# Ten rounds of both feed-forward gate and up products as seven block products of 256 tokens in place of eight

## The chip, the cores and the metric

The kernel runs on one core of one Trainium2 chip. Its time is device microseconds; that of the kernel before is 1849.38 us, the median of three runs from 1849.03 to 1849.63 us. The engines are TensorE (PE: matmuls, weight loads), VectorE (DVE), ScalarE (ACT), GpSimd (POOL) and the DMA queues, of which SyncE (SP) issues the weight loads. Each follows its own list of instructions, and semaphores tie the lists together.

## The reference

A first block of two token mixers is followed by a second block, in which two feed-forward layers enclose a hybrid mixer and a cross attention. There are 512 tokens of width 1024, in float32. What the change touches is the first half of both feed-forward layers:

```python
def swiglu(x, w_gate, w_up, w_down):
    return (jax.nn.silu(x @ w_gate) * (x @ w_up)) @ w_down
```

The argument `x` is the residual stream normed by its root mean square and scaled by a gain per feature; `w_gate` and `w_up` are 1024 x 2816. The output has the shape of the residual stream. In each of the two layers the gate and up products are 22 column tiles of 128 each.

## The kernel before, in words

All activations lie with features on the 128 partitions and tokens along the free dimension (512). A float32 product is made of three fp32r products: a number is a high part (rounded to fp32r) and a low part (the number less its high part), and high x high, high x low and low x high are summed in PSUM.

One round of the gate and up stage computes one gate tile and one up tile of 128 features: it loads 1 MB of weights (16 tiles of 128 x 128, eight of `w_gate` and eight of `w_up`) into one of two buffers `RAW`, in four units of four tiles. For each unit `split_unit` has GpSimd write the high part (L305) and the low part (L307) into one of four slots of `weights_hi` and `weights_lo`; a slot is free again once TensorE has used its unit. `feature_tile` on TensorE takes two units for the gate bank (L411 to L413: eight k-tiles, three products each, 512 columns) and two for the up bank, so a round has 48 products; rounds alternate between two pairs of PSUM banks. The pair of the first round is computed by `tile_pair`.

Behind TensorE, `dve_ffn_up` multiplies the gate bank (L1122) and the up bank (L1124) by the rms rows `RB`, ScalarE takes the silu of the gate (L1112), VectorE multiplies both (L1127), ScalarE rounds the result to its high part `Y_H` (L1114) and VectorE subtracts for the low part `Y_L` (L1129). The banks are free after L1122 and L1124. SP loads the weights of round r+2 into a buffer once all four low parts of round r are written (`units_ready`). There are 22 such rounds in each layer: about 596 to 838 us in the first, and 1476 to 1720 us in the second, with the products with `w_down` behind them.

At the head of the first layer, `dve_between` works out the rms rows and then norms the residual stream itself (L1480, eight instructions), and ScalarE writes `RB` (L576). At the head of the second, `RB` is written at the same place, and the first silu has to load an activation table first. The order of work is that of the program text on each engine; nothing plans it at run time.

## Time and profile before

| what | value |
|---|---|
| median of three runs | 1849.38 us |
| span of the profiled execution, first to last instruction | 1847.5 us |
| TensorE busy / its weight loads | 1821.5 us (99%) / 1491.6 us |
| GpSimd busy | 1257.9 us (68%) |
| VectorE busy / ScalarE busy | 885.0 us (48%) / 510.3 us (28%) |
| mean granted clock of TensorE | 0.996 of full speed |

The profiled execution has its span as its own time; no other total is given for it, and the median of the runs is 1.9 us above that span. A matmul's duration in the profile runs from its start to its modelled end and overlaps with the next one's, so the pace of TensorE is read from the distance of two starts and not from the duration.

### The profile page before, as it was taken

The page shows a single profiled execution, that of the slowest core. Times are in us where ns is not written, and L with a number is a line of the kernel's source. Part 1 is how long each engine was busy: PE and PEld are TensorE (multiplying, and loading weights), DVE is VectorE, ACT ScalarE, POOL GpSimd, SP SyncE. Part 2 cuts the span into 40 slices and gives each one's busy share as a digit, 9 for nine tenths or more (in the row PEclk, how much of TensorE's full clock was granted, in tenths as well). Part 3 has the DMA queues.
Part 4 walks back from the last instruction along what each step waited for, and adds up shares of the span by engine and source line. Part 5 has one row for each costly group of instructions (what it writes and reads, how often), then busy time and mean ns, then how long its engine had stood idle before and what let it go on. Part 6 is the DMA issues. An engine that isn't in the chain of part 4 may idle for free.

```text
span 1847.5 us, 25864 instructions
## 1 busy us (share of the span) xinstructions
PE 1821.5 (99%) x8940; PEld 1491.6 (81%) x8940; DVE 885.0 (48%) x1473; ACT 510.3 (28%) x947; POOL 1257.9 (68%) x1262
## 2 busy tenths in 40 slices
PE   9999999999999999999999999999999999999998
PEld 7888888878878788888888877798876778888886
DVE  5166663249974422224116767564444253333721
ACT  3111111137752111112014267554414231111001
POOL 7666666767777777777667865453771677777775
PEclk9999999999999999999999999999999999999999
DMA  5322223232213232223223211101330222222221
GB/s 185 104 82 89 91 91 137 94 123 91 85 68 115 97 109 95 91 99 126 94 80 115 96 65 46 69 26 46 114 114 24 91 80 91 96 108 91 99 107 68
DMA packets 25130, 170.48 MB, mean 92 GB/s; under 512 B 2784, under 2 KB 2912, under 8 KB 6496
## 3 DMA queue, kind: packets, MB, share of 16 engines
q1 hardware_dynamic: 23328, 159.92, 24.6%
q10 hardware_dynamic: 1728, 9.58, 1.4%
q8 instruction: 46, 0.75, 0.2%
q14 instruction: 28, 0.23, 0.0%
HBM read 167.39 MB, written 2.10 MB: 92 GB/s over the span
## 4 chain that ended last, share of the span: by engine, by line
PE 91%; DVE 3%; ACT 2%; POOL 2%; issue 1%; DMA 1%; DVEq 0%; ACTq 0%; POOLq 0%
PE bank L411 20%; PE bank L413 20%; PE bank L412 20%; PE bank L449 2%; PE bank L451 2%; PE bank L450 2%; PE bank L1324 2%; PE bank L1323 2%; PE bank L1322 2%; PE bank L1718 1%; POOL weights_lo L307 1%; PE bank L1994 1%; PE bank L1720 1%; PE bank L1719 1%; PE bank L2578 1%
## 5 line engine op out<-in xcount | busy, mean ns | idle before, releaser
L307 POOL TENSOR_TENSOR weights_lo<-raw_weights,weights_hi 128x512 fp32r<-128x512 f32 (+3 forms) x560 | 752.7, 1344 | 53.3 <-ACT weights_hi L326 7.5
L305 POOL TENSOR_SCALAR weights_hi<-raw_weights 128x512 fp32r<-128x512 f32 (+4 forms) x536 | 358.0, 668 | 433.9 <-PE bank L413 270.7
L411 PE MATMUL bank<-x_hi,weights_hi 128*128 128x512 f32 x1264 | 495.6, 392 | 0.2
L413 PE MATMUL bank<-x_lo,weights_hi 128*128 128x512 f32 x1264 | 492.0, 389 | 0.0
L412 PE MATMUL bank<-x_hi,weights_lo 128*128 128x512 f32 x1264 | 491.9, 389 | 0.0
L411 PEld LDWEIGHTS bank<-x_hi,weights_hi 128*128 128x128 f32 x1264 | 237.4, 188 | 50.5 <-issue 1.7
L413 PEld LDWEIGHTS bank<-x_lo,weights_hi 128*128 128x128 f32 x1264 | 237.3, 188 | 49.8
L412 PEld LDWEIGHTS bank<-x_hi,weights_lo 128*128 128x128 f32 x1264 | 237.4, 188 | 49.4 <-issue 1.0
L1124 DVE TENSOR_TENSOR temps<-bank,rms_rows 128x512 f32<-128x512 f32 x44 | 30.4, 690 | 185.7 <-PE bank L413 185.7
L1114 ACT ACTIVATE ffn_y_hi<-temps 128x512 f32 (+1 forms) x44 | 27.8, 633 | 239.7 <-DVE temps L1127 239.7
L1112 ACT ACTIVATE temps<-temps 128x512 f32<-128x512 f32 x44 | 27.8, 632 | 148.3 <-DVE temps L1122 148.3
L411 PE MATMUL bank<-ffn_y_hi,weights_hi 128*128 128x512 f32 x176 | 68.8, 391 | 0.0
L413 PE MATMUL bank<-ffn_y_lo,weights_hi 128*128 128x512 f32 x176 | 68.5, 389 | 0.0
L412 PE MATMUL bank<-ffn_y_hi,weights_lo 128*128 128x512 f32 x176 | 68.5, 389 | 0.0
L1322 PE MATMUL bank<-weights_hi,ffn_y_hi 128*128 128x512 f32 x176 | 68.5, 389 | 0.0
L1323 PE MATMUL bank<-weights_lo,ffn_y_hi 128*128 128x512 f32 x176 | 68.5, 389 | 0.0
L1324 PE MATMUL bank<-weights_hi,ffn_y_lo 128*128 128x512 f32 x176 | 68.5, 389 | 0.0
L1122 DVE TENSOR_TENSOR temps<-bank,rms_rows 128x512 f32<-128x512 f32 x44 | 30.4, 690 | 67.6 <-PE bank L413 64.8
L1129 DVE TENSOR_TENSOR ffn_y_lo<-temps,ffn_y_hi 128x512 f32 (+1 forms) x44 | 42.2, 958 | 42.5 <-ACT ffn_y_hi L1114 42.5
L449 PE MATMUL bank<-weights_hi,x_hi 128*128 128x512 f32 x156 | 61.8, 396 | 0.5 <-issue 0.5
L451 PE MATMUL bank<-weights_hi,x_lo 128*128 128x512 f32 x156 | 60.8, 389 | 0.0
L450 PE MATMUL bank<-weights_lo,x_hi 128*128 128x512 f32 x156 | 60.7, 389 | 0.0
(491 smaller groups left out, 3227.6 us busy)
## 6 DMA issues: line engine op xcount, KB each, us to landing
raw_weights<-in_ffn_up SPq DMA_DIRECT2D x44, 1024.0 KB, 4.8
raw_weights<-in_a_ug SPq DMA_DIRECT2D x16, 1024.0 KB, 4.8
raw_weights<-in_b_in SPq DMA_DIRECT2D x12, 1024.0 KB, 4.8
raw_weights<-in_ffn_down SPq DMA_DIRECT2D x8, 1408.0 KB, 6.0
raw_weights<-in_ffn_down SPq DMA_DIRECT2D x11, 1024.0 KB, 4.8
raw_weights<-in_a_out SPq DMA_DIRECT2D x8, 1024.0 KB, 4.7
raw_weights<-in_a_v SPq DMA_DIRECT2D x7, 1024.0 KB, 4.8
raw_weights<-in_b_out SPq DMA_DIRECT2D x8, 768.0 KB, 4.2
```

The source lines that it names most:

```text
L305: nc.gpsimd.tensor_scalar(hi, raw, 1.0, 0.0, ALU.mult, ALU.add).then_inc(S("units_hi"), 1)
L307: nc.gpsimd.tensor_tensor(lo, raw, hi.bitcast(F32), ALU.subtract).then_inc(units_ready, 1)
L411: nc.tensor.matmul(ps, wh, xh[:, k, :], start=k == 0, stop=False)
L412: nc.tensor.matmul(ps, wl, xh[:, k, :], start=False, stop=False)
L413: last = nc.tensor.matmul(ps, wh, xl[:, k, :], start=False, stop=k == last_k)
L449: nc.tensor.matmul(bank, xh[:, k, tok], wh, start=k == 0, stop=False)
L450: nc.tensor.matmul(bank, xh[:, k, tok], wl, start=False, stop=False)
L451: last = nc.tensor.matmul(bank, xl[:, k, tok], wh, start=False, stop=k == KD - 1)
L1129: nc.vector.tensor_tensor(Y_L[:, r, :], T[:, 3, :], Y_H[:, r, :].bitcast(F32), ALU.subtract).then_inc(S(f"{f}_yl"), 1)
L1322: nc.tensor.matmul(bank, Y_H[:, k, tok], wh, start=k == 0, stop=False)
L1323: nc.tensor.matmul(bank, Y_H[:, k, tok], wl, start=False, stop=False)
L1324: return nc.tensor.matmul(bank, Y_L[:, k, tok], wh, start=False, stop=k == KF - 1)
```

## The change

Of the 22 rounds of each layer, the first four and the last eight stay as they were; the ten between become a phase of their own. In it the round's product, 256 outputs (128 gate, 128 up) by 1024 inputs by 512 tokens, is seen as 2 x 2 blocks: outputs gate and up, inputs 0 to 511 and 512 to 1023, tokens 0 to 255 and 256 to 511. That is eight block products of four k-tiles by 256 tokens. The change computes them as seven (Winograd's form of Strassen's scheme), M1, M5, M6, M3, M7, M2, M4 in this order.

- Four of the seven weight blocks are sums or differences of units. VectorE makes them in each round (`dve_seven_sum`), in the buffers `SUMS`; the other three are units as loaded.
- Four of the seven activation blocks are differences of blocks of the gained residual stream. They are made once in each layer, during the first four rounds: ScalarE writes the gained stream (`act_gained`, eight instructions of 128 x 512), VectorE makes the four differences of 128 x 1024 (`dve_mix_x`), ScalarE rounds them to high parts, and VectorE and GpSimd make two low parts each.
- ScalarE now makes the seven high parts of the weights of a round (`act_seven_hi`) and GpSimd the seven low parts (`pool_seven`), each product with its own place in a ring of seven.
- Partial sums are kept and joined: ScalarE copies three half banks per round to SBUF (`act_keep`), and VectorE adds them back (`seven_joined`, `seven_gates`). Scaling, gating and splitting of the round's result are done as before, but in place in PSUM.
- SP loads the weights of a round r >= 2 of this phase once all seven low parts of round r-2 are written. The norming of the residual stream (L1480 before) is moved from the head of the first layer into the last eight rounds, the loads of `mem` and of the last gain behind the new phase, and the phase is written out in full instead of looped.

```diff
+HEAD, SEVEN, TAIL = 4, 10, 8
+PRODUCTS = 7
+POOL_LOWS = 7
...
-    Phase("ffn1_up", 22, 16), Phase("ffn1_down", 8, 22),
+    Phase("ffn1_up", HEAD, 16), Phase("ffn1_seven", SEVEN, 16, True), Phase("ffn1_tail", TAIL, 16), Phase("ffn1_down", 8, 22),
...
+                    if ph.seven and r >= 2:
+                        sp.wait_ge(*due("seven_lo", POOL_LOWS * (ph.sbase + r - 1)))
+                    elif ph.name.endswith("_tail") and r < 2:
+                        sp.wait_ge(*due("seven_lo", POOL_LOWS * (ph.sbase - 1 + r)))
+                    elif not (isinstance(r, int) and ph.base + r < 2):
+                        sp.wait_ge(units_ready, 4 * (ph.ubase - 1) + 4 * r)
...
+        def pe_bank_read(pe, f, g, which):
+            if g < 2:
+                return
+            if HEAD + 1 <= g < HEAD + SEVEN + 2:
+                pe.wait_ge(*due(f"{f}_{('sg', 'yl')[which]}", g - 1))
+            else:
+                pe.wait_ge(*due(f"{f}_{('tg', 'tu')[which]}", g - 1))
...
+            pe_seven(pe, f)
...
+        def pe_seven(pe, f):
+            ph = PH[f"{f}_seven"]
+            for r in range(SEVEN):
+                n, g = ph.sbase + r, HEAD + r
+                gate, up = PS[2 * (r % 2)], PS[2 * (r % 2) + 1]
+                def product(p, out, xh, xl, opens):
+                    pe.wait_ge(*due("seven_lo", POOL_LOWS * n + p + 1))
+                    for k in range(4):
+                        wh, wl = RING_HI[p][:, k, :], RING_LO[p][:, k, :]
+                        nc.tensor.matmul(out, wh, xh(k), start=opens and k == 0, stop=False, skip_group_check=True)
+                        nc.tensor.matmul(out, wl, xh(k), start=False, stop=False, skip_group_check=True)
+                        last = nc.tensor.matmul(out, wh, xl(k), start=False, stop=k == 3, skip_group_check=True)
+                    last.then_inc(S("seven_used"), 1)
+                def plain(x, first_k, half):
+                    return lambda k: x[:, first_k + k, half]
+                def mixed(x, p):
+                    return lambda k: x[:, MIX_OF[p], k, :]
+                pe_bank_read(pe, f, g, 1)
+                product(M1, up[:, A_HALF], plain(XH, 0, A_HALF), plain(XL, 0, A_HALF), True)
+                pe_bank_read(pe, f, g, 0)
+                if r == 0:
+                    pe.wait_ge(*due(f"{f}_mixed_lo_by_dve", 1))
+                product(M5, gate[:, B_HALF], mixed(MIX_H, M5), mixed(MIX_L, M5), True)
+                pe.wait_ge(*due("seven_kept", 3 * n + 1))
+                if r == 0:
+                    pe.wait_ge(*due(f"{f}_mixed_lo_by_dve", 2))
+                product(M6, up[:, A_HALF], mixed(MIX_H, M6), mixed(MIX_L, M6), False)
+                pe.wait_ge(*due("seven_kept", 3 * n + 2))
+                product(M3, gate[:, B_HALF], plain(XH, 4, B_HALF), plain(XL, 4, B_HALF), False)
+                pe.wait_ge(*due("seven_kept", 3 * n + 3))
+                if r == 0:
+                    pe.wait_ge(*due(f"{f}_mixed_lo_by_pool", 1))
+                product(M7, up[:, A_HALF], mixed(MIX_H, M7), mixed(MIX_L, M7), False)
+                product(M2, gate[:, A_HALF], plain(XH, 4, A_HALF), plain(XL, 4, A_HALF), True)
+                pe.wait_ge(*due("seven_joined", n + 1))
+                if r == 0:
+                    pe.wait_ge(*due(f"{f}_mixed_lo_by_pool", 2))
+                product(M4, up[:, A_HALF], mixed(MIX_H, M4), mixed(MIX_L, M4), False)
+        def pool_seven(pool, ph):
+            f = ph.name[:4]
+            for t in (2, 3):
+                pool.wait_ge(*due(f"{f}_mixed_hi", t + 1))
+                nc.gpsimd.tensor_tensor(MIX_L[:, t, :, :], MIX[:, t, :, :], MIX_H[:, t, :, :].bitcast(F32), ALU.subtract).then_inc(S(f"{f}_mixed_lo_by_pool"), 1)
+            for r in range(SEVEN):
+                for p in range(PRODUCTS):
+                    pool.wait_ge(*due("seven_hi", seven_count(ph, r, p)))
+                    nc.gpsimd.tensor_tensor(flat(RING_LO[p]), source_of(r, p), flat(RING_HI[p]).bitcast(F32), ALU.subtract).then_inc(S("seven_lo"), 1)
+        def act_gained(act, f, src, gain, ready):
+            for k in range(KD):
+                ready(k)
+                nc.scalar.activation(GX[:, k, :], src(k), ACT.Copy, scale=gain(k)).then_inc(S(f"{f}_gained"), 1)
+        def act_seven_hi(act, ph, r, p):
+            if r == 0:
+                if p < 4:
+                    act.wait_ge(units_used, PH[ph.name[:4] + "_up"].used(HEAD - 1, p))
+            else:
+                act.wait_ge(*due("seven_used", seven_count(ph, r - 1, p)))
+            if p == M1:
+                act.wait_ge(*due(f"raw{r % 2}", r // 2 * 16 + (8 * ph.base + 16 * (r % 2))))
+            if p in SUM_OF:
+                act.wait_ge(*due("seven_sums", 4 * (ph.sbase + r) + SUM_OF[p] + 1))
+            nc.scalar.activation(flat(RING_HI[p]), source_of(r, p), ACT.Copy).then_inc(S("seven_hi"), 1)
+        def act_silu(act, f, g, src):
+            act.wait_ge(*due(f"{f}_tg", g + 1))
+            nc.scalar.activation(T[:, 2, :], src, ACT.Silu).then_inc(S(f"{f}_sg"), 1)
+        def act_y_hi(act, f, g, src):
+            act.wait_ge(*due(f"{f}_y", g + 1))
+            nc.scalar.activation(Y_H[:, g, :], src, ACT.Copy).then_inc(S(f"{f}_yh"), 1)
+        def act_keep(act, ph, r, p, dst, bank):
+            act.wait_ge(*due("seven_used", seven_count(ph, r, p)))
+            nc.scalar.activation(dst, bank, ACT.Copy).then_inc(S("seven_kept"), 1)
+        def act_ffn_up(act, f, after_seven):
+            ph = PH[f"{f}_seven"]
+            for g in range(2):
+                act_silu(act, f, g, T[:, 0, :])
+                act_y_hi(act, f, g, T[:, 3, :])
+            for t in range(4):
+                act.wait_ge(*due(f"{f}_mixed", t + 1))
+                nc.scalar.activation(MIX_H[:, t, :, :], MIX[:, t, :, :], ACT.Copy).then_inc(S(f"{f}_mixed_hi"), 1)
+            for g in range(2, HEAD - 1):
+                act_silu(act, f, g, T[:, 0, :])
+                act_y_hi(act, f, g, T[:, 3, :])
+            for p in range(M4):
+                act_seven_hi(act, ph, 0, p)
+            for r in range(SEVEN):
+                g, more = HEAD + r, r + 1 < SEVEN
+                gate, up = PS[2 * (r % 2)], PS[2 * (r % 2) + 1]
+                old_gate, old_up = PS[2 * (1 - r % 2)], PS[2 * (1 - r % 2) + 1]
+                act_silu(act, f, g - 1, old_gate)
+                act_seven_hi(act, ph, r, M4)
+                act_keep(act, ph, r, M1, KEPT[:, A_HALF], up[:, A_HALF])
+                if more:
+                    act_seven_hi(act, ph, r + 1, M1)
+                act_keep(act, ph, r, M5, KEPT5, gate[:, B_HALF])
+                if more:
+                    act_seven_hi(act, ph, r + 1, M5)
+                act_y_hi(act, f, g - 1, old_up)
+                act_keep(act, ph, r, M6, KEPT[:, B_HALF], up[:, A_HALF])
+                if more:
+                    for p in (M6, M3, M7, M2):
+                        act_seven_hi(act, ph, r + 1, p)
+            last = HEAD + SEVEN - 1
+            act_silu(act, f, last, PS[2 * (last % 2)])
+            act_y_hi(act, f, last, PS[2 * (last % 2) + 1])
+            after_seven(act)
+            for g in range(HEAD + SEVEN, KF):
+                act_silu(act, f, g, T[:, 0, :])
+                act_y_hi(act, f, g, T[:, 3, :])
...
+        def dve_mix_x(dve, f):
+            dve.wait_ge(*due(f"{f}_gained", KD))
+            for t, (x, y) in enumerate(((GX[:, FIRST, B_HALF], GX[:, FIRST, A_HALF]), (GX[:, OTHER, B_HALF], MIX[:, 0, :, :]),
+                                        (GX[:, OTHER, B_HALF], GX[:, FIRST, B_HALF]), (GX[:, OTHER, A_HALF], MIX[:, 1, :, :]))):
+                if t in (1, 3):
+                    dve.wait_ge(*due(f"{f}_mixed", t // 2 + 1))
+                nc.vector.tensor_tensor(MIX[:, t, :, :], x, y, ALU.subtract).then_inc(S(f"{f}_mixed"), 1)
+        def dve_mixed_low(dve, f, t):
+            dve.wait_ge(*due(f"{f}_mixed_hi", t + 1))
+            nc.vector.tensor_tensor(MIX_L[:, t, :, :], MIX[:, t, :, :], MIX_H[:, t, :, :].bitcast(F32), ALU.subtract).then_inc(S(f"{f}_mixed_lo_by_dve"), 1)
+        def dve_seven_sum(dve, ph, r, p):
+            n = ph.sbase + r
+            if p == M5:
+                dve.wait_ge(*due(f"raw{r % 2}", r // 2 * 16 + (8 * ph.base + 16 * (r % 2))))
+                x, y, op = unit_of(r, 2), unit_of(r, 3), ALU.add
+            elif p == M6:
+                dve.wait_ge(*due("seven_sums", 4 * n + 1))
+                x, y, op = sum_of(M5), unit_of(r, 0), ALU.subtract
+            elif p == M3:
+                dve.wait_ge(*due("seven_sums", 4 * n + 2))
+                x, y, op = unit_of(r, 1), sum_of(M6), ALU.subtract
+            else:
+                x, y, op = unit_of(r, 0), unit_of(r, 2), ALU.subtract
+            if r:
+                dve.wait_ge(*due("seven_lo", POOL_LOWS * (n - 1) + p + 1))
+            nc.vector.tensor_tensor(sum_of(p), x, y, op).then_inc(S("seven_sums"), 1)
...
+        def dve_ffn_up(dve, step, f, in_tail):
+            head, ph, tail = PH[f"{f}_up"], PH[f"{f}_seven"], PH[f"{f}_tail"]
+            dve_ffn_plain(dve, f, head, 0, 0)
+            dve_ffn_plain(dve, f, head, 1, 1)
+            dve_mix_x(dve, f)
+            dve_ffn_plain(dve, f, head, 2, 2)
+            dve_mixed_low(dve, f, 0)
+            dve_mixed_low(dve, f, 1)
+            dve.wait_ge(*due(f"{f}_yl", HEAD - 1))
+            for p in (M5, M6, M3, M7):
+                dve_seven_sum(dve, ph, 0, p)
+            last_head = HEAD - 1
+            dve.wait_ge(units_used, head.used(last_head, 1))
+            dve_gate_scaled(dve, f, PS[2 * (last_head % 2)])
+            for r in range(SEVEN):
+                g, n, more = HEAD + r, ph.sbase + r, r + 1 < SEVEN
+                gate, up, old_up = PS[2 * (r % 2)], PS[2 * (r % 2) + 1], PS[2 * (1 - r % 2) + 1]
+                dve_up_ready(dve, f, g - 1)
+                dve_up_scaled(dve, f, old_up)
+                if more:
+                    dve_seven_sum(dve, ph, r + 1, M5)
+                dve_gated(dve, f, g - 1, old_up)
+                if more:
+                    dve_seven_sum(dve, ph, r + 1, M6)
+                    dve_seven_sum(dve, ph, r + 1, M3)
+                dve_gated_low(dve, f, g - 1, old_up)
+                if more:
+                    dve_seven_sum(dve, ph, r + 1, M7)
+                dve.wait_ge(*due("seven_used", seven_count(ph, r, M7)))
+                dve.wait_ge(*due("seven_kept", 3 * n + 2))
+                nc.vector.tensor_tensor(up[:, B_HALF], up[:, A_HALF], KEPT5, ALU.add).then_inc(S("seven_joined"), 1)
+                dve.wait_ge(*due("seven_used", seven_count(ph, r, M2)))
+                dve.wait_ge(*due("seven_kept", 3 * n + 3))
+                nc.vector.tensor_tensor(gate, gate, KEPT, ALU.add).then_inc(S("seven_gates"), 1)
+                dve.wait_ge(*due("seven_gates", n + 1))
+                dve_gate_scaled(dve, f, gate)
+            last = HEAD + SEVEN - 1
+            old_up = PS[2 * (last % 2) + 1]
+            dve_up_ready(dve, f, last)
+            dve_up_scaled(dve, f, old_up)
+            dve_gated(dve, f, last, old_up)
+            dve_gated_low(dve, f, last, old_up)
+            for r in range(TAIL):
+                dve_ffn_plain(dve, f, tail, r, HEAD + SEVEN + r)
+                in_tail(r)
...
-            for k in range(KD):
-                last = nc.vector.scalar_tensor_tensor(out=X[:, k, :], in0=X[:, k, :], scalar=vec("normf", k), in1=PS[6], op0=ALU.mult, op1=ALU.mult)
-            last.then_inc(S("x2"), 1)
-            dve.wait_ge(*due("s2b_rb", 1))
+            nc.vector.scalar_tensor_tensor(out=X[:, k, :], in0=X[:, k, :], scalar=vec("normf", k), in1=PS[6], op0=ALU.mult, op1=ALU.mult).then_inc(S("x2"), 1)
+            act_gained(act, "ffn1", lambda k: X[:, k, :], lambda k: NG[:, k:k + 1], lambda k: act.wait_ge(*due("b_x", KD)) if k == 0 else None)
+                act_gained(act, "ffn2", lambda k: X[:, k, :], lambda k: vec("ffn2_pre", k), lambda k: act.wait_ge(*due("kept_x", len(JOIN_BANK))) if k == 0 else None)
```

## Rows read from the trace of the kernel before

**Rows 1.** The page, parts 1 and 4: busy time, then the chain by engine.

```profile
PE 1821.5 (99%) x8940; PEld 1491.6 (81%) x8940; DVE 885.0 (48%) x1473; ACT 510.3 (28%) x947; POOL 1257.9 (68%) x1262
...
PE 91%; DVE 3%; ACT 2%; POOL 2%; issue 1%; DMA 1%; DVEq 0%; ACTq 0%; POOLq 0%
```

**Rows 2.** Windows, one plain round: length, busy PE PEld DVE ACT POOL, clock, DMA.

```profile
1513.60:1524.50 10.90, 10.90 (x50) 9.03 (x49) 2.78 (x4) 1.26 (x2) 8.33 (x8) 1.00 0.27 98
```

**Rows 3.** Timeline of TensorE, 512 columns (start, duration, engine, line).

```profile
700.38 0.39 PE L411 MATMUL bank<-x_hi,weights_hi 128*128 128x512 f32 x1
...
701.06 0.39 PE L411 MATMUL bank<-x_hi,weights_hi 128*128 128x512 f32 x1
```

**Rows 4.** Timeline of TensorE, 256 columns: first and last of 48 products.

```profile
959.08 0.28 PE L411 MATMUL bank<-mem_key_hi,weights_hi 128*128 128x256 f32 x1
...
964.72 0.28 PE L413 MATMUL bank<-mem_key_lo,weights_hi 128*128 128x256 f32 x1
```

**Rows 5.** Timeline of GpSimd, low parts whose high part is ready.

```profile
961.57 2.65 POOL L307 TENSOR_TENSOR weights_lo<-raw_weights,weights_hi 128x512 fp32r<-128x512 f32 x2 [0.23 <-ACT weights_hi L326]
```

**Rows 6.** Timeline of VectorE and GpSimd, first feed-forward, VectorE starts first.

```profile
697.99 0.69 DVE L1127 TENSOR_TENSOR temps<-temps 128x512 f32<-128x512 f32 x1
698.05 1.78 POOL L307 TENSOR_TENSOR weights_lo<-raw_weights,weights_hi 128x512 fp32r<-128x512 f32 x1
699.66 0.72 DVE L1129 TENSOR_TENSOR ffn_y_lo<-temps,ffn_y_hi 128x512 f32 x1 [0.98 <-ACT ffn_y_hi L1114]
700.06 0.80 POOL L305 TENSOR_SCALAR weights_hi<-raw_weights 128x512 fp32r<-128x512 f32 x1 [0.23 <-PE bank L413]
...
703.49 1.29 POOL L307 TENSOR_TENSOR weights_lo<-raw_weights,weights_hi 128x512 fp32r<-128x512 f32 x1
```

**Rows 7.** The same in the second feed-forward, GpSimd starts first.

```profile
1547.53 1.29 POOL L307 TENSOR_TENSOR weights_lo<-raw_weights,weights_hi 128x512 fp32r<-128x512 f32 x1
1547.59 1.77 DVE L1127 TENSOR_TENSOR temps<-temps 128x512 f32<-128x512 f32 x1 [0.25 <-DVE temps L1124]
```

**Rows 8.** Source view of four lines: min/median/max ns, first and last start.

```profile
L1112 ACT ACTIVATE temps<-temps x44: 632/632/633, 620.6 to 1716.1; 128x512 f32<-128x512 f32 x44
L1528 ACT ACTIVATE mem_key_hi<-mem_key_raw x8: 417/418/421, 871.9 to 875.2; 128x256 fp32r<-128x256 f32 x8
L1540 DVE TENSOR_TENSOR mem_key_lo<-mem_key_raw,mem_key_hi x8: 409/674/2067, 875.1 to 881.4; 128x256 fp32r<-128x256 f32 x8
L1122 DVE TENSOR_TENSOR temps<-bank,rms_rows x44: 677/691/692, 619.8 to 1715.3; 128x512 f32<-128x512 f32 x44
```

**Rows 9.** Timeline, VectorE and ScalarE at the start of both feed-forwards.

```profile
614.56 5.36 DVE L1480 SCALAR_TENSOR_TENSOR residual<-residual,vecs,bank 128x512 f32<-128x512 f32 x8 [0.62 <-PE bank L490]
615.42 0.60 ACT L576 ACTIVATE rms_rows<-bank 128x512 f32<-128x512 f32 x1 [18.00 <-PE bank L490]
...
627.15 0.69 DVE L1129 TENSOR_TENSOR ffn_y_lo<-temps,ffn_y_hi 128x512 fp32r<-128x512 f32 x1 [0.70 <-ACT ffn_y_hi L1114]
631.90 0.69 DVE L1124 TENSOR_TENSOR temps<-bank,rms_rows 128x512 f32<-128x512 f32 x1 [3.46 <-PE bank L413]
...
1501.96 1.28 ACT L1112 ACT_TABLE_LOAD   x1
1503.26 0.63 ACT L1112 ACTIVATE temps<-temps 128x512 f32<-128x512 f32 x1
1509.94 1.70 DVE L1129 TENSOR_TENSOR ffn_y_lo<-temps,ffn_y_hi 128x512 fp32r<-128x512 f32 x1 [0.70 <-ACT ffn_y_hi L1114]
1514.02 0.69 DVE L1124 TENSOR_TENSOR temps<-bank,rms_rows 128x512 f32<-128x512 f32 x1 [1.77 <-PE bank L413]
```

**Rows 10.** Timeline of TensorE, then windows: a pause of TensorE and the clock behind it.

```profile
1471.01 1.22 PE L490 MATMUL bank<-temps,ones 128*128 128x512 f32 x1 [2.17 <-DVE temps L539]
...
1470.00:1480.00 10.00, 7.68 (x13) 4.35 (x14) 7.45 (x12) 4.78 (x9) 5.51 (x6) 0.50 0.30 105
```

**Rows 11.** The page, part 6: weight loads (KB each, us to landing).

```profile
raw_weights<-in_ffn_up SPq DMA_DIRECT2D x44, 1024.0 KB, 4.8
```

171 lines of the change are left out of this document (111 added, 60 removed).

## The prediction

> **What bounds the kernel now.** I read the page first: TensorE is busy 99% of the span and holds 91% of the chain that ended last, GpSimd is busy 68% [rows 1]. So time is won only by giving TensorE less to do, and only if nobody makes it wait. In one plain round of 10.9 us TensorE is busy throughout, GpSimd for 8.33 us, VectorE for 2.78 and ScalarE for 1.26 [rows 2]. TensorE's pace I read from starts in the timeline. A k-tile of three products of 512 columns takes 701.06 - 700.38 = 0.68 us, so 48 products take 16 x 0.68 = 10.88 us [rows 3]. The same code has one stage with 256 columns: the last of 48 products starts 5.64 us behind the first, 5.64 / 47 = 0.120 us each, weight loads included [rows 4].
>
> **What the change removes: TensorE's work.** A round of seven has 7 x 4 x 3 = 84 products of 256 columns, 84 x 0.120 = 10.08 us against 10.88. That is 0.80 us a round and 16.0 us over 20 rounds, no more, since half the columns cost more than half the time. I take no loss from the waits between products: the 48 of rows 4 had such a wait every twelve, and kept this pace.
>
> **What it adds to GpSimd, in steady rounds.** GpSimd loses its high parts and gets seven low parts. Two low parts in a row, both ready, take 2.65 us in all, 1.29 each and 0.07 between; so one is 1.36 and seven are 9.5 us [rows 5]. That would fit in 10.08. But VectorE now makes four weight sums per round from two SBUF operands, and such instructions get in GpSimd's way. In rows 6 L1127 (two SBUF operands) runs from 697.99 to 698.68 at its full pace and the low part issued 0.06 us later takes 1.78 instead of 1.29, so 0.49 lost; the high part beside L1129 takes 0.80 [rows 6]. In rows 7 GpSimd was 0.06 us first: now it takes 1.29, and L1127 takes 1.77 instead of 0.69, because it ends only 0.54 us behind GpSimd's end at 1548.82 [rows 7]. Operations with one operand in PSUM, as L1122, show a steady 0.69 [rows 8]. So the two take turns, one instruction at a time. Where GpSimd is never idle, a sum waits for the end of the low part, then runs 0.54 us; the next low part would have been issued 0.07 into that. In rows 6 the low part ends 1.15 us behind the end of the VectorE instruction, so here it ends 0.54 + 1.15 = 1.69 behind the last one instead of 1.36, a loss of 0.33. Four sums cost 1.3 us (2.0 at the 0.49 of rows 6). GpSimd's round is 9.5 + 1.3 = 10.8 us, with the upper end 11.5.
>
> The Trainium skill says the same of the two engines (SBUF — State Buffer, "Who interferes with whom"): a VectorE instruction with two SBUF inputs contends with a GpSimd instruction that reads SBUF, and whoever comes first holds the pair for its whole instruction. By rows 6 and 7 the order of issue does decide, but the loser loses 0.33 to 0.49 us and not the full 0.69; by the rule's full 0.69 a GpSimd round would be 9.5 + 2.8 = 12.3 us.
>
> So GpSimd, not TensorE, sets the later rounds. It starts each phase with some lead, because a product's place in the ring is free as soon as TensorE has used it. At 10.08 us per round TensorE eats 0.7 us of lead a round. The lead has a second claim on it: weights of round r+2 are ordered only behind the last low part of round r and land 4.8 us later [rows 11], and VectorE's first sum of r+2 wants them at the start of round r+1. I reckon three rounds at 10.08 and then six at 10.8, 6 x 0.7 = 4.5 per layer, **+9 us** for both (0 at the least; at 11.5 for all of these rounds, 6 x 1.4 x 2 = +17). VectorE's own list has three places per round where its delay reaches TensorE. It needs 6 x 0.69 + 0.41 + 4 x (0.54 to 1.69), some 9.1 us in the middle [rows 8], and its joined half must be there before M4; that is tight but not behind GpSimd. ScalarE has 9 x 0.63 + 3 x 0.42 = 6.9 us [rows 8] and is not late in steady rounds.
>
> **What it adds at the start of each phase.** This is the largest term. The activation differences, their high and low parts and the sums of the first round hang on one chain on VectorE, mixed with the rounds before. For a piece of 128 x 1024 no row exists. On VectorE 256 columns take 0.41 and 512 take 0.69, so I take 1.25; on ScalarE 0.42 and 0.63 give 1.06; on GpSimd 2 x 1.29 less some overhead give 2.5. Bounds: a single 512 piece, and twice the 512 piece with a wait of 2.5 for the other engine.
>
> Second layer. Before, the first silu runs at 1503.26, behind the table load, and the second round's low part ends at 1511.64 [rows 9]. Now eight gained copies (8 x 0.6 = 4.9) stand before the table load, in the way of the silu, so that low part ends about 1516.5. Four differences, 5.1: 1521.7. The third round's scaling, gating and low part (L1124 showed its bank ready at 1514.0) follow only now, with ScalarE's four wide high parts and a wide GpSimd piece in their way, 6.1: 1527.8. Two wide low parts with one wait, 3.5: 1531.3. Four sums with two waits, 5.2: 1536.5. Then the fourth round's gate is scaled, 0.7, its silu runs, M4's high part, and only then the copy of M1, in ScalarE's order of program, 0.63 + 0.63 + 0.42 and 0.9 of handing over: 1539.8. M6 may not start before it. Without a stall the phase would start at 1513.6 + 10.9 = 1524.5 and M6 2.9 later, at 1527.4. TensorE is **12.5 us** late.
>
> First layer. The gained copies lie in an idle stretch of ScalarE that ends with the wait of 18.00 us before L576, and L1480's 5.36 us are gone from VectorE's list. The second round's low part ended at 627.84 [rows 9], and now can at about 625.6. The differences collide with GpSimd's splits of the fourth round, 4 x 1.9: 633.2. Third round 4.8: 638.0. Wide low parts, each behind a wide GpSimd piece, 6.9: 644.9. Sums 6.1, scaling 0.7, ScalarE's three 2.6: 654.3. M6 without a stall: 631.5 + 10.9 + 2.9 = 645.3. **9 us** late.
>
> Bounds for both together: if none of these turns cost anything (each chain less all waits on GpSimd), the first is about 1.5 late and the second about 6.5, 8 together; with each wide piece waiting for a wide one, some 30. I take 21.5, since rows 7 show the wait nearly each time the two meet.
>
> **The clock.** After a pause of 2.17 us TensorE's granted clock reads 0.50, its lower level of 1.2 GHz, over the 10 us behind it [rows 10]. The start stalls above are pauses of 3 to 5 us, broken by single products. A product at half clock takes 1.44 more; three or four per start are 4 to 6 us, but the lead that GpSimd gains meanwhile takes back most of what the later rounds lose. Net I take **+2** for both (0 to +8). The Trainium skill also has idle TensorE falling to half clock (TensorE: Matmul & The Clock Gate, "What's actually happening"); the trace agrees with its 0.50, and the sum uses only the row.
>
> **Costed at nothing.** The norming moved into the last eight rounds (0.69 a round where VectorE is idle over 7 us per round), the later loads of `mem` and gain, the written-out loop, and the change back to plain rounds: units 0 to 3 are free as the last round's M1 to M3 finish, and GpSimd then needs 8 of 10.9 us. If GpSimd is late there, one split of 2 us shows, less the 1.4 us of M4: under 1 us a layer.
>
> **Sum.** Against the profiled execution, whose own time is its span of 1847.5 us: -16.0 + 9.0 + 21.5 + 2.0 = +16.5 us, 1864.0. The runs' median is 1.9 above that span, and I carry it over: **1866 us**, 0.9% slower.
>
> **Rivals.**
> - TensorE keeps what it saves. VectorE and GpSimd hinder each other little, the start stalls are the 8 us of the lower bound and all rounds take 10.08: -16 + 8 = -8, 1841 us. For it speaks GpSimd's 9.5 us of bare work; against it rows 6 and 7, which show the turns in every plain round. This ends on the other side; it decides where four sums cost GpSimd less than 0.6 us per round. 0.15.
> - The turns cost more. Sum, low part and late weights fall into a pattern in which each low part loses 0.49 or more, or by the rule quoted above a whole VectorE instruction: rounds of 11.5 to 12.3. With +17 to +26 for the +9 and 22 at the starts: -16 + 22 + 22 + 2 = +30, 1879 us. For it: VectorE's list leaves 1 us free, so a wait there reaches M4 through the joined half. Against: GpSimd's lead grows whenever TensorE waits. 0.20.
> - Most of the start chains is hidden but the steady rounds are GpSimd's: starts 10, rounds +9, no clock loss: +3, 1852 us. 0.13.
>
> **Chances.** The forecast (1857 to 1873) has 0.52. The measurement of this kernel can't tell less than 0.2%, 3.7 us, from no change. Faster than 1845.7: the first rival and a little, 0.15. Within: from the third rival, 0.09. Slower: 0.76. The range is 1846 to 1885: it leaves out the first rival and the far end of the second.
>
> **What would show it.** TensorE's starts 0.120 apart inside a product; a phase of ten rounds near 108 us behind its first; M6 of the first round late by 9 and 12.5 us, with VectorE's chain in front; VectorE sums of up to 1.8 us and low parts of up to 1.8; GpSimd over 95% busy from the fourth round on. Wrong would be low parts of 1.29 beside the sums, or first rounds no longer than 13 us.

## The result, and the profile after

The changed kernel takes 1856.99 us (median of four runs, 1856.92 to 1861.75), the kernel before 1849.39 us in the same comparison. The ratio is 1.0046, with an interval from 1.0033 to 1.0059: 7.6 us slower. Forecast were 1866 us, 16.5 slower. The range (1846 to 1885) held the time; of the band that the forecast itself was given, 1857 to 1873, it is the lower edge.

The profiled execution is the longest of the four, 1861.75 us with a span of 1859.9. It reached the feed-forward stages 3.5 us later than before (its second round of the first layer starts at 610.49 instead of 606.95), in stages that the change doesn't touch. It fell behind between 20 and 30 us, where TensorE's clock was at its lower level for a part (granted clock is the third figure from the end; kernel before, then changed kernel):

```profile
20.00:30.00 10.00, 10.00 (x48) 8.42 (x49) 7.81 (x27) 0.21 (x1) 8.51 (x10) 1.00 0.45 161
20.00:30.00 10.00, 9.68 (x33) 8.01 (x34) 6.99 (x31) 0.21 (x1) 6.33 (x7) 0.66 0.48 180
```

Another 1.0 us came between the two layers. So I compare stages and not spans. From TensorE's first product of the second round of a layer to its first product with `w_down`, the starts in the two timelines give

| layer | before | after | difference |
|---|---|---|---|
| first | 606.95 to 838.42: 231.46 us | 610.49 to 844.60: 234.11 us | +2.65 |
| second | 1489.82 to 1720.54: 230.72 us | 1497.02 to 1732.99: 235.97 us | +5.25 |

Together +7.9 us, within 0.3 us of what the medians show. Of the page after, the lines that answer to [rows 1], and three groups of the new work (part 5: busy, mean ns, idle before):

```profile
PE 1818.1 (98%) x9660; PEld 1520.4 (82%) x9660; DVE 1013.5 (54%) x1605; ACT 628.5 (34%) x1171; POOL 1319.8 (71%) x1246
...
PE 77%; POOL 9%; DVE 7%; ACT 3%; issue 2%; DMA 1%; DVEq 0%; ACTq 0%; POOLq 0%
...
L1225 POOL TENSOR_TENSOR weights_lo<-temps,weights_hi 128x512 fp32r<-128x512 f32 x60 | 78.8, 1340 | 5.0 <-ACT weights_hi L1244 5.0
...
L1225 POOL TENSOR_TENSOR ring_lo<-raw_weights,ring_hi 128x512 fp32r<-128x512 f32 x40 | 67.2, 1699 | 0.0
...
L1338 DVE TENSOR_TENSOR temps<-raw_weights 128x512 f32<-128x512 f32 x40 | 50.9, 1272 | 19.2 <-DMA raw_weights<-in_ffn_seven 19.2
```

TensorE has a little less to do than before and is no longer the chain: 77% in place of 91%, and GpSimd and VectorE hold 16%. The low parts of the sevens come in two kinds, 1340 and 1699 ns on average.

Where the 7.9 us lie is read from the starts of M1, one per round. The differences of these starts, in us, worked out from the timeline of TensorE:

```
round             0      1      2      3      4      5      6      7      8
first layer   13.94  10.14  10.58  10.58  10.55  10.58  10.57  10.56  11.82
second layer  16.88  10.08  10.08  10.46  10.59  10.55  11.83  10.08  10.08
```

The tenth round takes 10.08 us in both layers. A round of undisturbed TensorE is 10.08 us, as forecast. I use two figures per layer from here on. The *start* is the delay of the first M1 plus what round 0 takes above 10.08. When that M1 is due, 35.50 and 34.79 us behind the second round's start, I take from the experiment e5 below, in which it was not held up. The *steady rest* is what the rounds behind take above 10.08 each. After, the starts are 2.14 + 3.86 = 6.0 us and 3.4 + 6.8 = 10.2 us, the rests 4.7 and 3.1, together 7.85. With 20 x 0.80 saved: -16.0 + 16.2 + 7.85 = +8.05 against the 7.9 measured.

Windows of the changed kernel (length, busy time of PE, PEld, DVE, ACT, POOL, clock, DMA share, GB/s): the start of the first layer, a steady round of it, the start of the second layer, an early round of it. They answer to [rows 2].

```profile
645.99:662.07 16.08, 13.36 (x86) 12.68 (x85) 15.16 (x16) 8.93 (x17) 14.72 (x10) 0.79 0.11 35
693.37:703.92 10.55, 10.32 (x86) 10.12 (x85) 8.55 (x10) 6.35 (x13) 10.55 (x8) 1.00 0.28 98
1531.83:1552.09 20.26, 13.75 (x85) 13.06 (x85) 18.69 (x18) 9.46 (x19) 16.64 (x11) 0.75 0.13 42
1562.17:1572.25 10.08, 10.08 (x86) 10.08 (x85) 8.78 (x11) 6.22 (x12) 10.08 (x7) 1.00 0.24 81
```

In the steady round GpSimd is busy without a gap, and it is so in the early one too, where TensorE is still on time: that one lives on GpSimd's lead, the low parts that it has finished before TensorE wants them. The clock reads 0.79 and 0.75 over the starts.

In the late rounds TensorE doesn't wait for a low part. It waits before the last product, M4, for the joined half (L1394), which stands behind the sum for M7 in VectorE's list:

```profile
712.96 0.39 PE L1183 MATMUL bank<-x_mixed_hi,ring_hi 128*128 128x256 f32 x1 [0.24 <-DVE bank L1394]
```

So the delay reaches TensorE through VectorE. Which of the two engines makes it is what the experiments have to tell.

### The profile page after: what moved, and what is told of

It is laid out like the page before. It is cut to its first block, busy times and chain, and to the rows that moved or that the text cites. A ratio compares the mean times of both kernels' runs of the same rounds, so it can differ in the third digit from the quotient of the medians.

```text
span 1859.9 us, 26686 instructions
## 1 busy us (share of the span) xinstructions
PE 1818.1 (98%) x9660; PEld 1520.4 (82%) x9660; DVE 1013.5 (54%) x1605; ACT 628.5 (34%) x1171; POOL 1319.8 (71%) x1246
## 4 chain that ended last, share of the span: by engine, by line
PE 77%; POOL 9%; DVE 7%; ACT 3%; issue 2%; DMA 1%; DVEq 0%; ACTq 0%; POOLq 0%
PE bank L436 15%; PE bank L437 15%; PE bank L438 15%; POOL weights_lo L1225 4%; POOL ring_lo L1225 4%; PE bank L1602 2%; PE bank L1601 2%; PE bank L474 2%; PE bank L1600 2%; PE bank L476 2%; PE bank L475 2%; PE bank L2002 1%; PE bank L2278 1%; PE bank L2004 1%; PE bank L2003 1%
## 5 line engine op out<-in xcount | busy, mean ns | idle before, releaser
L329 POOL TENSOR_TENSOR weights_lo<-raw_weights,weights_hi 128x512 fp32r<-128x512 f32 (+3 forms) x480 | 644.1, 1342 | 46.6 <-ACT weights_hi L348 7.9
L327 POOL TENSOR_SCALAR weights_hi<-raw_weights 128x512 fp32r<-128x512 f32 (+3 forms) x456 | 306.4, 672 | 380.3 <-PE bank L438 213.1
L436 PE MATMUL bank<-x_hi,weights_hi 128*128 128x512 f32 x944 | 371.1, 393 | 0.2
L438 PE MATMUL bank<-x_lo,weights_hi 128*128 128x512 f32 x944 | 367.5, 389 | 0.0
L437 PE MATMUL bank<-x_hi,weights_lo 128*128 128x512 f32 x944 | 367.4, 389 | 0.0
L436 PEld LDWEIGHTS bank<-x_hi,weights_hi 128*128 128x128 f32 x944 | 177.3, 188 | 37.9 <-POOL weights_lo L329 0.8
L438 PEld LDWEIGHTS bank<-x_lo,weights_hi 128*128 128x128 f32 x944 | 177.2, 188 | 37.1
L437 PEld LDWEIGHTS bank<-x_hi,weights_lo 128*128 128x128 f32 x944 | 177.3, 188 | 36.9 <-issue 1.0
L1225 POOL TENSOR_TENSOR weights_lo<-temps,weights_hi 128x512 fp32r<-128x512 f32 x60 | 78.8, 1340 | 5.0 <-ACT weights_hi L1244 5.0
L1225 POOL TENSOR_TENSOR ring_lo<-raw_weights,ring_hi 128x512 fp32r<-128x512 f32 x40 | 67.2, 1699 | 0.0
L1338 DVE TENSOR_TENSOR temps<-raw_weights 128x512 f32<-128x512 f32 x40 | 50.9, 1272 | 19.2 <-DMA raw_weights<-in_ffn_seven 19.2
L1591 POOL TENSOR_TENSOR weights_lo<-raw_weights,weights_hi 128x512 fp32r<-128x512 f32 x44 | 57.1, 1297 | 3.7
```

The source lines that it names most:

```text
L327: nc.gpsimd.tensor_scalar(hi, raw, 1.0, 0.0, ALU.mult, ALU.add).then_inc(S("units_hi"), 1)
L329: nc.gpsimd.tensor_tensor(lo, raw, hi.bitcast(F32), ALU.subtract).then_inc(units_ready, 1)
L436: nc.tensor.matmul(ps, wh, xh[:, k, :], start=k == 0, stop=False)
L437: nc.tensor.matmul(ps, wl, xh[:, k, :], start=False, stop=False)
L438: last = nc.tensor.matmul(ps, wh, xl[:, k, :], start=False, stop=k == last_k)
L1225: nc.gpsimd.tensor_tensor(flat(RING_LO[p]), source_of(r, p), flat(RING_HI[p]).bitcast(F32), ALU.subtract).then_inc(S("seven_lo"), 1)
```

## The experiments

The table has all kernels in the same figures (us; first layer and second layer). Kernels marked * leave out or replace part of the computation. Starts and rests are those of one profiled execution each; ratios are to the kernel before in the same comparison, where its median was 1849.35 to 1849.88 us.

| kernel | median | starts | steady rests | ratio to before, interval |
|---|---|---|---|---|
| changed kernel | 1856.99 | 6.0, 10.2 | 4.7, 3.1 | 1.0046 (1.0033 to 1.0059) |
| e1 sums from PSUM * | 1846.99 | 3.2, 10.5 | 0, 0 | 0.9981 (0.9971 to 0.9990) |
| e2 weights never late * | 1855.76 | 5.4, 11.3 | 3.9, 1.5 | 1.0033 (1.0020 to 1.0045) |
| e9 both * | 1845.59 | 3.2, 9.4 | 0, 0 | 0.9982 (0.9972 to 0.9991) |
| e4 two rounds of seven | 1861.71 | 5.4, 10.2 | - | 1.0066 (1.0049 to 1.0083) |
| e3 gained copies first | 1855.16 | 5.3, 7.2 | 5.4, 4.1 | 1.0029 (1.0018 to 1.0041) |
| e5 no mixed activations * | 1843.88 | 0.4, 0.4 | 4.5, 3.6 | 0.9970 (0.9959 to 0.9982) |
| e6 six rounds ahead | 1846.89 | 1.2, 2.8 | 3.3, 3.3 | 0.9985 (0.9976 to 0.9995) |
| e7 M7's low part by VectorE | 1849.68 | 5.5, 9.5 | 0, 0.1 | 1.0002 (0.9993 to 1.0012) |
| e8 e3, e6 and e7 together | 1839.68 | 1.4, 1.8 | 0.5, 0 | 0.9945 (0.9931 to 0.9959) |

**The steady rounds: whose are they?** In the trace after, VectorE's first sum of a steady round is put down to the weight load (19.2 us in all in part 5), and GpSimd is full at the same time. Two theories: the turns of VectorE and GpSimd make the rounds long, or the weights arrive too late. Three kernels tell them apart.

```diff
 e1
-            nc.vector.tensor_tensor(sum_of(p), x, y, op).then_inc(S("seven_sums"), 1)
+            nc.vector.tensor_tensor(sum_of(p), PS[7], y, op).then_inc(S("seven_sums"), 1)
```

> The first operand of the four weight sums comes from a PSUM bank in place of SBUF (so the sums are not the block sums, and the output is not the reference's); count, shapes, order and waits are those of the changed kernel. Theory, turns of VectorE and GpSimd: no sum has two SBUF operands any more, low parts fall from 1.29/1.74 us to 1.29, seven need 9.3 us, and rounds fall from 10.57 to 10.1 us; the first round of each phase gets 1 to 3 us shorter too; 1846 to 1849 us in all, against 1857. Rival, late weight loads: GpSimd's turns are a symptom, VectorE's first sum still waits for the load, rounds stay at 10.4 us or more, 1855 us or more.

```diff
 e2, in the SyncE loads, for rounds r >= 2 of the sevens
-                        sp.wait_ge(*due("seven_lo", POOL_LOWS * (ph.sbase + r - 1)))
...
+                        if r >= 4:
+                            sp.wait_ge(*due("seven_lo", POOL_LOWS * (ph.sbase + r - 3)))
...
+                        sp.dma_start(RAW[:, parity, 20:22, :].rearrange("p t n -> p (t n)"), src[r][:, 0:2 * P]).then_inc(S(f"raw{parity}"), 16)
+                        return
```

> From round 2 of each phase of sevens on, only 128 KB are loaded, beside the buffer, and not behind the low parts, so that the weights of rounds 0 and 1 are used again (the output is not the reference's). VectorE's first sum of a round then never waits for a load. Theory, turns of VectorE and GpSimd: GpSimd is full all the same, rounds stay at 10.5 to 10.6 us, 1856 to 1857 us. Rival, late weight loads: rounds fall to 10.1 us and the time to 1849 us.

> Both edits together: sums with one PSUM operand and no late weights (output not the reference's). Theory, turns: as with the sums alone, rounds of 10.08 us. If the sums alone leave a rest above 10.08 that this takes away, the loads had a share. What is left above the kernel before is the start of both phases: 1849.4 - 16.0 + 13 = 1846 us.

e1 gave 1846.99 us, e2 1855.76, e9 1845.59. In e1 every round behind round 0 takes 10.08 us in both layers; in e2 the late ones still take 10.58 to 10.59. A round of e1 (windows), then its low parts and sums (min/median/max ns):

```profile
697.96:708.04 10.08, 10.08 (x86) 10.08 (x85) 6.29 (x11) 6.21 (x12) 9.00 (x8) 1.00 0.28 105
```

```profile
L1225 POOL TENSOR_TENSOR ring_lo<-raw_weights,ring_hi x40: 1290/1297/1367, 651.5 to 1625.9; 128x512 fp32r<-128x512 f32 x40
...
L1338 DVE TENSOR_TENSOR temps<-bank,raw_weights x60: 676/680/692, 645.0 to 1619.5; 128x512 f32<-128x512 f32 x60
```

The same views of the changed kernel:

```profile
L1225 POOL TENSOR_TENSOR weights_lo<-temps,weights_hi x60: 1278/1295/1776, 649.3 to 1637.3; 128x512 fp32r<-128x512 f32 x60
L1225 POOL TENSOR_TENSOR ring_lo<-raw_weights,ring_hi x40: 1287/1743/1767, 655.7 to 1641.1; 128x512 fp32r<-128x512 f32 x40
L1225 POOL TENSOR_TENSOR weights_lo<-raw_weights,weights_hi x20: 1703/1741/2237, 645.7 to 1633.1; 128x512 fp32r<-128x512 f32 x20
L1225 POOL TENSOR_TENSOR ring_lo<-temps,ring_hi x20: 1289/1742/1760, 654.0 to 1638.5; 128x512 fp32r<-128x512 f32 x20
...
L1338 DVE TENSOR_TENSOR temps<-raw_weights x40: 680/1186/1816, 646.8 to 1632.5; 128x512 f32<-128x512 f32 x40
```

With a PSUM operand in the sums all medians of low parts are 1297 to 1306 ns and a sum takes 680; with two SBUF operands three of four groups of low parts stand at 1741 to 1743, and a sum takes up to 1816. GpSimd goes from 10.55 us busy of 10.55 to 9.00 of 10.08. Nothing else was changed, so the turns of the two engines make the steady rest, all 7.85 us of it. What e1 leaves open is whether GpSimd's full list or VectorE's makes the round, since it shortens both; e7 below settles that. The round is GpSimd's arithmetic. Its low parts in the changed kernel:

```profile
701.40 1.74 POOL L1225 TENSOR_TENSOR weights_lo<-raw_weights,weights_hi 128x512 fp32r<-128x512 f32 x1
703.10 3.80 POOL L1225 TENSOR_TENSOR weights_lo<-temps,weights_hi 128x512 fp32r<-128x512 f32 x3
706.85 1.75 POOL L1225 TENSOR_TENSOR ring_lo<-temps,ring_hi 128x512 fp32r<-128x512 f32 x1
```

A low part beside a sum keeps the next one off for 1.70 us (701.40 to 703.10), one by itself for 1.25 (703.10 to 706.85 are three of them). Four and three of these are 10.55.

One expectation of e1 failed. Its start got 2.8 us shorter in the first layer, but in the second it stayed: 10.5 for 10.2.

The load is a follower. In a round of e2 the DMA share falls to 0.06, and GpSimd is still busy for all of it:

```profile
702.00:712.59 10.59, 10.49 (x87) 10.18 (x86) 9.22 (x10) 6.23 (x13) 10.59 (x8) 1.00 0.06 16
```

What the loads do cost is small: e2's rests are 2.4 us shorter, without the rounds of 11.82 that stand once in each layer of the changed kernel, and its starts 0.5 us longer. (In a round of 11.82 VectorE's first sum waits longest for its weights, 2.08 us before 1606.91 in the second layer. e1, which loads as the changed kernel does, has no such round.) Against the changed kernel e2 is 1.2 us shorter, less than this measurement tells from no change; e9 against e1 is 1.4.

**The starts: how much, and what makes them?**

```diff
 e4
-HEAD, SEVEN, TAIL = 4, 10, 8
+HEAD, SEVEN, TAIL = 4, 2, 16
```

> The phase of sevens has two rounds in place of ten, and 16 plain rounds follow. It keeps the whole start of a phase and hardly anything of its steady rounds. Theory, the start chain costs 6.0 and 10.2 us as the trace of the changed kernel shows: 1849.4 + 16.2 - 4 x 0.8 = 1862 us, slower than with ten rounds. Rival, the loss is spread over the ten rounds and a shorter phase loses less: 1853 us or less.

1861.71 us, as expected to 0.3 us: the starts stand by themselves, and with only two rounds to earn them back the kernel is slower still. Windows of round 0 in both layers:

```profile
644.90:658.24 13.34, 11.90 (x84) 11.44 (x85) 11.95 (x15) 8.90 (x17) 12.13 (x8) 0.87 0.07 14
1531.50:1548.40 16.90, 13.54 (x84) 12.98 (x85) 15.34 (x17) 8.91 (x17) 13.43 (x9) 0.70 0.17 53
```

```diff
 e5: the gained copies, differences, their high and low parts and the waits for them are gone
-                    return lambda k: x[:, MIX_OF[p], k, :]
+                    return lambda k: (XH if x is MIX_H else XL)[:, MIX_OF[p] % 2 * 4 + k, A_HALF if MIX_OF[p] < 2 else B_HALF]
...
-            dve_mix_x(dve, f)
...
-            dve_mixed_low(dve, f, 0)
-            dve_mixed_low(dve, f, 1)
```

> The differences of the activation blocks are left out, with the gained copies, their high and low parts and the waits for them; the products that used them take plain halves of the activations (output not the reference's). The sums of the first round stay. Theory, the chain of the differences is the start cost: starts fall from 6.0 and 10.2 us to 0 to 1.5 each, steady rounds stay at 10.57; 1842 to 1844 us. Rival, the first round's sums and ScalarE's order hold TensorE by themselves: at least 6 of the 16 us stay, 1848 us or more.

1843.88 us; the profiled execution is the shortest of seven, 1841.56, and the longest took 1847.19. The starts fall from 16.2 to 0.8 us, the first M1 is no longer late, and round 0 takes 10.49 us at full clock:

```profile
642.78:653.27 10.49, 10.32 (x86) 10.12 (x85) 8.24 (x10) 7.53 (x15) 9.58 (x7) 1.00 0.21 63
```

So the first round's sums hold nobody up by themselves; the chain of the differences does. In the first layer the turns that the sums take lengthen that chain, as e1 shows; without it they are hidden. The rests stay at 4.5 and 3.6, as they should by the first finding.

```diff
 e3
+                act_gained(act, "ffn2", ...)
                 act_rows(act, "s5", PS[6], RB[:, :])
-                act_gained(act, "ffn2", ...)
```

> One reordering on ScalarE in the second layer: the eight gained copies run before the copy of the rms rows, where ScalarE waits, and no longer between it and the first silu. Everything is computed. Theory: the start chain of the second layer begins 4.9 us sooner, and its start costs 5 to 6 us in place of 10.2; 1852 us against 1857. Rival, the chain is held by VectorE's and GpSimd's turns further down and not by where it begins: under 2 us gained.

1855.16 us: a miss by 3 us. The second layer's start fell by 3.0 us and not by the 4.9 at which I had put the eight copies, and 1.0 came back in its steady rest, 4.1 for 3.1. The chain did begin 4.9 us sooner (first silu at 1505.83, 13.4 us behind the second round's start and not 18.4). But the four differences now fall beside GpSimd's splits of the fourth round and take 7.7 us in place of 5.9, and M6 of round 0 is late by 6.8 us in place of 8.8. So 2.0 us of the 3.0 are the chain's; the rest is clock, since half as many products of round 0 run at the lower level. That 1.0 came back is the lesson: a late start gives GpSimd time ahead, and a start made shorter uncovers rounds that are GpSimd's. The first layer shows the same trade without any edit: the code is that of the changed kernel there, its start is 0.7 us shorter and its rest 0.7 longer, and the layer takes 234.16 us for 234.11. What was different there is the clock, 1.00 and not 0.79 over the same stretch:

```profile
642.88:658.31 15.43, 10.78 (x86) 10.27 (x86) 14.05 (x16) 8.90 (x17) 14.07 (x9) 1.00 0.05 8
```

**What comes of it.** Both causes have a cure that computes everything.

```diff
 e6
-HEAD, SEVEN, TAIL = 4, 10, 8
+HEAD, SEVEN, TAIL = 6, 8, 8
...
             dve_ffn_plain(dve, f, head, 1, 1)
-            dve_mix_x(dve, f)
+            dve_mix_x(dve, f, (0, 1))
             dve_ffn_plain(dve, f, head, 2, 2)
+            dve_mix_x(dve, f, (2, 3))
+            dve_ffn_plain(dve, f, head, 3, 3)
             dve_mixed_low(dve, f, 0)
             dve_mixed_low(dve, f, 1)
+            dve_ffn_plain(dve, f, head, 4, 4)
```

ScalarE's high parts of the differences follow the same order. Eight rounds of seven is what the place of the differences allows here: it is that of the last eight tiles of `Y_H` and `Y_L`.

> Six plain rounds ahead, eight rounds of seven, eight plain ones behind; the differences are spread over the plain rounds, two at a time, and their low parts lie two rounds before the phase. Everything is computed. Only 16 rounds are of seven: -12.8 us. Theory: starts cost 0 to 2 us each, the rounds behind the third 10.57: -12.8 + 2 + 5 = -6, 1843.5 us, faster than both kernels. Rival, a start costs the same wherever it lies: -12.8 + 16 + 5, 1857 us or more.

1846.89 us: faster than both kernels, if only by 2.5 us than the one before (0.15%, with no change just outside the interval), and 3.4 us short of what I expected. Starts are 1.2 and 2.8 us, but the rounds are GpSimd's from round 1 on (10.86, then 10.57) and not from the fourth, and round 0, in which GpSimd is busy throughout, seems to leave no lead. Windows of rounds 0 and 1:

```profile
664.47:675.75 11.28, 10.34 (x86) 10.13 (x85) 9.96 (x12) 7.65 (x15) 11.28 (x8) 1.00 0.05 9
675.75:686.61 10.86, 10.33 (x87) 10.12 (x86) 8.38 (x11) 6.37 (x13) 10.86 (x8) 1.00 0.33 124
```

```diff
 e7
-POOL_LOWS = 7
+POOL_LOWS = 6
...
-            return SUMS[:, SUM_OF[p], :]
+            return PS[4] if p == M7 else SUMS[:, SUM_OF[p], :]
...
+        def dve_m7_low(dve, ph, r):
+            dve.wait_ge(*due("seven_hi", seven_count(ph, r, M7)))
+            nc.vector.tensor_tensor(flat(RING_LO[M7]), sum_of(M7), flat(RING_HI[M7]).bitcast(F32), ALU.subtract).then_inc(S("seven_lo_by_dve"), 1)
```

> The sum for M7 is written to a free PSUM bank and its low part is taken by VectorE (one SBUF operand), so GpSimd has six low parts. Everything is computed. Theory: GpSimd needs 6 x 1.32 + 4 x 0.33 = 9.2 us and rounds fall to 10.1; the starts stay at about 16 us: 1849 us. Rival: VectorE, at 8.6 us of 10.55 and now 0.7 more, becomes late with the joined half before M4, rounds stay at 10.4 us or more and the time at 1855.

1849.68 us, 0.7 us from the expected. A steady round of it takes 10.08 us. VectorE is busy for 8.72 us of it, more than the 8.55 of a late round of the changed kernel, and its joined half is in time; GpSimd has 9.39. So it was GpSimd's list that was too long, and VectorE only passed the delay on.

```profile
698.48:708.56 10.08, 10.08 (x86) 10.08 (x85) 8.72 (x12) 6.18 (x12) 9.39 (x7) 1.00 0.29 104
```

> The three working edits together: six plain rounds ahead with the differences spread over them, the gained copies of the second layer ahead of the rms rows, and M7's low part by VectorE. Everything is computed. Theory: 16 rounds of seven at 10.08 us take away 12.8 us; no steady round is GpSimd's any more; the starts cost 1 to 2 us each: 1839 to 1841 us, faster than both kernels and than each edit alone (1846.9 and 1849.7). Rival: the parts do not add up, since GpSimd's lead and the start stalls stand in for each other; 1844 us or more.

1839.68 us, ratio 0.9945 (0.9931 to 0.9959): 10.2 us faster than the kernel before, 17.3 than the changed one. The parts add up: -12.8 + 3.2 + 0.5 = -9.1, and the rest of 1.1 us lies within the interval, 2.6 us to either side. Two rounds of it; in the second GpSimd is still busy throughout, yet TensorE is on time:

```profile
696.66:706.74 10.08, 10.08 (x86) 10.08 (x85) 8.71 (x12) 6.18 (x12) 9.61 (x7) 1.00 0.31 106
1573.53:1583.61 10.08, 10.08 (x86) 10.08 (x85) 8.79 (x12) 6.18 (x12) 10.08 (x8) 1.00 0.30 105
```

## Why the prediction was right, point by point

**TensorE's saving, -16.0 us: right.** Rounds of 10.08 us stand in every kernel in which nobody was late, 0.120 us per product.

**Steady rounds, +9 us: right in mechanism, measured +7.85, and the size in part by luck.** GpSimd's round was put at 10.8 and is 10.55, but not as the sum had it. A low part by itself takes 1.25 us from start to start and not 1.36, 0.8 us less for seven; and each of the four sums costs 0.45 (1.70 for 1.25) and not 0.33, 0.5 us more. The two errors cancel in part. The 1.36 came from a pair of which the second may not have been ready: its high part ends at 962.79, 0.07 us before the first low part, and the second starts at 962.93.

```profile
962.16 0.63 ACT L326 ACTIVATE weights_hi<-raw_weights 128x512 fp32r<-128x512 f32 x1 [0.76 <-PE bank L413]
```

The 1.32 and 0.33 in the expectation of e7 split the same 10.56 wrongly too. And 6 x 0.7 is 4.2, where the prediction wrote 4.5. The place was half right: the delay reaches TensorE at the joined half before M4, which the prediction called tight but not behind GpSimd. The number of rounds at 10.08 first (three forecast; one and two measured) also depends on how late the start is.

**Starts, +21.5 us: right in place and order, too large.** This is the term that made 1866 out of 1857. It was forecast as the lateness of M6 in round 0, 9 and 12.5 us; M6 starts 5.3 us (654.18) and 8.8 us (1543.53) late, 14.1 in all. So the term was 7.4 us too large. (The starts of the table, 16.2 us, also hold what round 0 loses behind M6.) The chain in the second layer, VectorE first:

```profile
1521.73 0.69 DVE L1307 TENSOR_TENSOR ffn_y_lo<-temps,ffn_y_hi 128x512 fp32r<-128x512 f32 x1 [0.70 <-ACT ffn_y_hi L1252]
1522.34 2.31 DVE L1316 TENSOR_TENSOR x_mixed<-gained_x 128x1024 f32<-128x1024 f32 x1
...
1531.88 2.07 DVE L1307 TENSOR_TENSOR ffn_y_lo<-temps,ffn_y_hi 128x512 fp32r<-128x512 f32 x1 [0.70 <-ACT ffn_y_hi L1252]
1533.88 3.41 DVE L1320 TENSOR_TENSOR x_mixed_lo<-x_mixed,x_mixed_hi 128x1024 fp32r<-128x1024 f32 x2
1537.21 0.68 DVE L1338 TENSOR_TENSOR temps<-raw_weights 128x512 f32<-128x512 f32 x1
1537.93 0.69 DVE L1338 TENSOR_TENSOR temps<-temps,raw_weights 128x512 f32<-128x512 f32 x1
1538.65 0.69 DVE L1338 TENSOR_TENSOR temps<-raw_weights,temps 128x512 f32<-128x512 f32 x1
1539.26 1.76 DVE L1338 TENSOR_TENSOR temps<-raw_weights 128x512 f32<-128x512 f32 x1
1540.94 0.69 DVE L1341 TENSOR_TENSOR bank<-bank,rms_rows 128x512 f32<-128x512 f32 x1
```

ScalarE:

```profile
1509.05 5.01 ACT L1231 ACTIVATE gained_x<-residual,vecs 128x512 f32<-128x512 f32 x8
1514.07 1.28 ACT L1248 ACT_TABLE_LOAD   x1
...
1537.98 2.08 ACT L1244 ACTIVATE weights_hi<-temps 128x512 fp32r<-128x512 f32 x3 [5.62 <-DVE temps L1338]
...
1542.11 0.58 ACT L1248 ACTIVATE temps<-bank 128x512 f32<-128x512 f32 x1
1542.59 0.62 ACT L1244 ACTIVATE ring_hi<-raw_weights 128x512 fp32r<-128x512 f32 x1
1543.11 0.37 ACT L1256 ACTIVATE temps<-bank 128x256 f32<-128x256 f32 x1
```

Up to the second round's low part it is what I had: eight copies of 5.01 us, the table load, and an end at 1522.4, which is 1515.2 on the clock of the trace before (7.2 us are the shift of the second layer): forecast 1516.5. The wide pieces were right too: 1.22 us alone and 2.31 behind a GpSimd instruction. The 3.41 at 1533.88 are the two low parts together (2.28 and 1.21); they end at 1537.3, 1530.1 for 1531.3. What failed is the sums and what is behind them. Three of the four sums meet no GpSimd instruction and take 0.69 each, so that the four end at 1541.0 (forecast 1543.7 on this clock). Then I added ScalarE's silu, high part and copy at full length each; the starts in the rows lie 0.48 and 0.52 us apart, not 0.63 plus a hand-over, and the copy of M1 is done at 1543.5, forecast 1547.0. I had treated each waiting pair as a turn: right where both engines have work in front of them, wrong where GpSimd itself waits for the high parts of these sums (it is idle for 3.62 us before 1538.69). A turn needs both sides. In the first layer the 3.7 us too many lie in the same places: 1.6 up to the end of the wide low parts, 1.3 in the sums, 0.8 behind them.

**The clock, +2 us: right, as far as the runs can tell.** TensorE in the second start:

```profile
1535.22 0.36 PE L1183 MATMUL bank<-x_hi,weights_hi 128*128 128x256 f32 x1 [3.23 <-POOL weights_lo L1225]
...
1540.61 0.55 PE L1183 MATMUL bank<-x_mixed_hi,weights_hi 128*128 128x256 f32 x1 [3.27 <-POOL weights_lo L1225]
...
1541.39 0.41 PE L1183 MATMUL bank<-x_mixed_hi,weights_hi 128*128 128x256 f32 x1
1541.61 0.41 PE L1184 MATMUL bank<-x_mixed_hi,weights_lo 128*128 128x256 f32 x1
...
1543.53 0.58 PE L1183 MATMUL bank<-x_mixed_hi,weights_hi 128*128 128x256 f32 x1
```

M5's products start 0.213 to 0.22 us apart, where 0.120 is the pace at full clock: the lower of the two levels, as the clock of 0.75 over this window says. From its first product to M6's first are 2.92 us, where 1.44 is the full pace. Yet most of this is hidden. M6 waits for the copy of M1, which ends at 1543.48 in a run of ScalarE's without a gap, whatever TensorE's pace. The other kernels bear it out. In the first layer M6 is 5.3 us late in the changed kernel and in e2, e3, e4 and e7; of these e3 and e7 ran M1, M5 and M6 at 0.120 (but for the first step behind a wait), and the others ran 12 to 24 of these products at the lower level. In the second layer it is 8.8 us late in the changed kernel, e2, e4 and e7. So what the clock adds to the start is what stands behind M6: 6.0 - 5.3 = 0.7 and 10.2 - 8.8 = 1.4 us, 2.1 in all (0.1 to 0.7 and 0.7 to 2.4 in these kernels). Of that the steady rest gives some back, in the first layer all, as e3 shows. M6's lateness and clock together were forecast at 23.5 us, and are 16.2.

**Costed at nothing: right.** The tail shows no stall at the change back (its eight rounds take 87.1 us in both layers, 8 x 10.88 = 87.0), and nothing of the norming, the moved loads or the written-out loop shows in TensorE's starts.

**The rivals.** The first, in which TensorE keeps all it saves, is what e1, e7 and e9 make of the kernel by force, and it falls only by the turns and the starts. The second put a turn at 0.49 us or more, up to the full length of VectorE's instruction; the Trainium skill's words for it (SBUF — State Buffer, "Who interferes with whom": whoever issues first gets the shared ports for the whole instruction, and the other fully blocks) describe what a wide low part of VectorE suffers in the first layer, 3.41 us for 1.22 behind one of GpSimd's, but a low part that is next in line loses 0.45 of a sum's 0.69 us. The page writes the sentence on the whole instruction of VectorE's two-port modes; of two SBUF inputs it says that they contend, without a price. The third, at 1852, had the starts at 10 us. The measured time lies between it and the forecast, and nearer to it: 5 us from it and 9 from 1866. Of the signs of being wrong that the prediction named, none came: low parts beside the sums read 1.74 and not 1.29, and the first rounds took 13.9 and 16.9 us.
